# A routed two-layer block on one Trainium2 core: router logits taken from rows before their normalization

## The reference, cut to what matters

```python
def layer_norm(x, g, b):                       # float32
    mu = jnp.mean(xf, axis=-1, keepdims=True)
    var = jnp.mean(jnp.square(xf - mu), axis=-1, keepdims=True)
    y = (xf - mu) * lax.rsqrt(var + LN_EPS)
    return (y * g + b).astype(x.dtype)

# first block, for i in (0, 1); 256 tokens, D = 1024
h = x * (1.0 + sc_m) + sh_m
y = conformer_conv(h, ...) if i == 0 else short_gated_conv(h, ...)
x = layer_norm(ALPHA * x + (1.0 + g_m) * y, mix_ln_g[i], mix_ln_b[i])
h = x * (1.0 + sc_f) + sh_f
y = hierarchical_moe(h, ...)                   # 4 groups of 8 experts, D_EXPERT = 512
x = layer_norm(ALPHA * x + (1.0 + g_f) * y, ffn_ln_g[i], ffn_ln_b[i])

# hierarchical_moe
g_logits = xf @ w_group + b_group              # 4 columns
g_idx    = argmax(g_logits)
e_logits = (xf @ w_router + b_router)          # 32 columns, the 8 of the group are kept
top_p, top_e = lax.top_k(e_probs, 2)
# every expert: (silu(x @ w_gate) * (x @ w_up)) @ w_down, weighted and summed per token
```

## Time and profile before

| | us |
|---|---|
| median of 3 runs (2533.52 to 2539.37) | 2539.05 |
| span of the profiled execution, core 0 | 2539.9 |
| PE busy | 2433.0 (96%) |
| DVE busy | 1417.5 (56%) |
| ACT busy | 886.7 (35%) |
| POOL busy | 306.5 (12%) |
| PE's part of the chain that ended last | 74% |
| DMA's part of that chain | 15% |

### The profile page before, as it was taken

One profiled execution on the slowest core, in us unless ns is written; L12 is line 12 of the kernel. 1 busy time (PEld: TensorE's weight loads), 2 busy tenths in 40 slices (PEclk: granted clock), 3 DMA queues, 4 the chain that ended last, 5 costly groups with the idle time before them and its releaser, 6 DMA issues.

```text
span 2539.9 us, 37572 instructions
## 1 busy us (share of the span) xinstructions
PE 2433.0 (96%) x14976; PEld 1750.8 (69%) x14977; DVE 1417.5 (56%) x2512; ACT 886.7 (35%) x1560; POOL 306.5 (12%) x371
## 2 busy tenths in 40 slices
PE   7999999998999999998999999999999999999998
PEld 4664444443686444443488899988888889998887
DVE  6564323322666333323366785767677678576767
ACT  2241111111342111111144465454444446555443
POOL 0210001000000001000000122430010012243001
PEclk8999999999999999999999999999999999999999
DMA  9979999999887999999947563443743856345381
GB/s 396 380 307 418 419 420 419 419 419 419 293 302 296 408 420 419 419 420 419 399 138 269 164 192 115 140 169 127 271 166 127 271 163 190 114 140 171 123 274 52
DMA packets 246338, 710.44 MB, mean 280 GB/s; under 512 B 11794, under 2 KB 165138, under 8 KB 189586
## 3 DMA queue, kind: packets, MB, share of 16 engines
q1 hardware_dynamic: 243810, 704.94, 73.0%
q10 hardware_dynamic: 2352, 3.06, 0.4%
HBM read 705.46 MB, written 1.05 MB: 278 GB/s over the span
## 4 chain that ended last, share of the span: by engine, by line
PE 74%; DMA 15%; DVE 5%; issue 3%; ACT 2%; POOL 1%; SPq 0%; DVEq 0%; ACTq 0%; POOLq 0%
DMA ring<-in_e_w_up_dram 12%; PE w L1271 12%; PE y L1057 11%; PE w L1050 11%; PE w L975 8%; PE w L1289 6%; PE w L1049 6%; PE w L978 4%; PE w L1552 2%; PE w L1252 1%; PE y L1325 1%; PE y L876 1%; DVE wsp L1662 1%; PE y L1496 1%; ACT wsp L1652 1%
## 5 line engine op out<-in xcount | busy, mean ns | idle before, releaser
L1662 DVE TENSOR_TENSOR wsp<-ring,wsp 128x1024 fp32r<-128x1024 f32 x452 | 558.2, 1243 | 253.0 <-ACT wsp L1652 251.9
L1652 ACT CAST wsp<-ring 128x1024 fp32r<-128x1024 f32 x452 | 468.5, 1047 | 297.5 <-PE w L1050 99.4
L1271 PE MATMUL w<-ring,arena 128*64 128x512 f32 x2048 | 465.0, 601 | 47.3 <-DMA ring<-in_e_w_up_dram 45.0
L1271 PEld LDWEIGHTS w<-ring,arena 128*64 128x64 f32 x2048 | 151.1, 138 | 314.6 <-issue 308.0
L1050 PE MATMUL w<-hx,wsp 128*128 128x512 f32 x1344 | 348.2, 391 | 0.0
L1050 PEld LDWEIGHTS w<-hx,wsp 128*128 128x128 f32 x1344 | 246.9, 189 | 44.6
L975 PE MATMUL w<-hx,wsp 128*128 128x256 f32 x1984 | 266.2, 287 | 1.5 <-ACT arena L2801 1.1
L975 PEld LDWEIGHTS w<-hx,wsp 128*128 128x128 f32 x1984 | 248.4, 193 | 16.9 <-issue 12.3
L1057 PE MATMUL y<-wsp,zsp 128*128 128x512 f32 x1008 | 245.1, 392 | 2.9 <-POOL zsp L2910 1.7
L2164 DVE TENSOR_TENSOR ht<-w,ht 128x256 f32<-128x256 f32 x64 | 39.5, 618 | 370.8 <-ACT ht L2710 370.8
L2710 ACT ACTIVATE ht<-w 128x256 f32<-128x256 f32 x64 | 40.0, 626 | 586.7 <-PE w L1271 586.7
(11 more groups left out here) (351 smaller groups left out, 2938.7 us busy)
## 6 DMA issues: line engine op xcount, KB each, us to landing
ring<-in_e_w_gate_dram SPq DMA_DIRECT2D x128, 1024.0 KB, 13.6
ring<-in_e_w_up_dram SPq DMA_DIRECT2D x128, 1024.0 KB, 15.5
ring<-in_e_w_down_dram SPq DMA_DIRECT2D x112, 1024.0 KB, 13.6
ring<-in_ffn_in_dram SPq DMA_DIRECT2D x88, 1024.0 KB, 6.9
ring<-in_ada_w_dram SPq DMA_DIRECT2D x48, 1024.0 KB, 14.4
ring<-in_w_in_dram SPq DMA_DIRECT2D x48, 1024.0 KB, 5.4
ring<-in_ffn_out_dram SPq DMA_DIRECT2D x44, 1024.0 KB, 6.9
ring<-in_b_w_in_dram SPq DMA_DIRECT2D x12, 1024.0 KB, 12.2
```

Of the source, the lines that this page charges most:

```text
L1271: ins = pe.matmul(b[64 * c:64 * c + 64, :], xg[:, u, kc, x0:x0 + CAP], r4[:, k, :, 256 * c:256 * c + 256], start=kc == 0, stop=kc == KC - 1)
L1652: ac.copy(shaped(halves(i)[0], u.shape), u.cut(ring[:, u.piece % NSLOT, :])).then_inc(*mark("w_high", i))
L1662: ve.tensor_tensor(shaped(lo, u.shape), u.cut(ring[:, u.piece % NSLOT, :]), shaped(hi, u.shape).bitcast(F32), ALU.subtract).then_inc(*mark ...
```

## The change

Four things are rewritten, in both layers.

1. **Logits from raw rows.** PE transposes `vv` as soon as the residual has been added, not when it is normalized. The products with the 40 router columns then give logits of raw rows. With s and c the column sums (`router_sums`, 9 matmuls with 2 rows out) copied over all partitions (`router_rows`, 2 matmuls), logits are repaired on DVE by `base` = s * (-mean * rstd) + c and `fixed` = raw * rstd + `base`. The bias row's matmul for each block is gone. Scales of features (`router_scale`, the 16 small matmuls) stand behind the logits.
2. **Who normalizes.** DVE does no longer normalize; ACT does, as activation with scale and bias, two halves a block, followed by the two high parts of the block. Pool makes -mean * rstd behind each power, and then all four low parts. DVE has no `row_low` any more.
3. **DVE's order.** All four half rows are first gated and added, then statistics are taken. The steps of the choice of block 0 and 1 alternate. `negatives` is one instruction for a block. Of the scaling steps, `gathered(0, 1)` stands ahead of `token_weights`.
4. **PE's fillers.** In layer 0 no `ada(1,1,kc)` stands ahead of `moe(0)`: kc 0 and 1 stand behind the router, kc 2 to 4 behind the ranks of block 0, kc 5 to 7 behind the counts. In layer 1 `keep_busy` of 2, 5 and 4 stands at these places, and the one between the two blocks is gone.

The core of the diff:

```diff
             def router(l, n):
+                def turn_rows(t, h):
+                    pe.wait_ge(*at("norm_v", n, "added", t, h))
+                    for q in range(4):
+                        f = 4 * h + q
+                        ins = pe.transpose(WB[2 * t + h][:, q * P:(q + 1) * P], vv[:, t, f * P:(f + 1) * P], ident)
+                    ins.then_inc(*mark("route_pe", "turned", l, t, h))
+                turn_rows(0, 0)
+                turn_rows(0, 1)
+                router_sums(l, n)
+                turn_rows(1, 0)
+                router_rows(l)
+                turn_rows(1, 1)
...
+                router_scale(l)
...
                 if l == 0:
-                    for kc in range(4, 6):
+                    for kc in range(2):
                         ada(1, 1, kc)
                 else:
-                    keep_busy(WB[0], 4)
+                    keep_busy(WB[0], 2)
+                pe.wait_ge(*at("route_v", l, "oo", 0))
+                pe.matmul(b[:, 0:32], tri, oo[:, 0, :], start=True, stop=True).then_inc(*mark("route_pe", "ranks", l, 0))
+                if l == 0:
+                    for kc in range(2, 5):
+                        ada(1, 1, kc)
+                else:
+                    keep_busy(WB[0], 5)
...
-            router_shift(0)
-            for kc in range(4):
-                ada(1, 1, kc)
...
+                def base(t):
+                    ve.wait_ge(*at("route_s", "rows", l))
+                    ve.wait_ge(*at("shifted", n, t))
+                    step("base", t, lambda: ve.scalar_tensor_tensor(route_base[:, t, :], route_rows[:, 0, :], nm[:, t:t + 1],
+                                                                    route_rows[:, 1, :], ALU.mult, ALU.add))
...
+                def scaled(t, h):
+                    if h == 0:
+                        ac.wait_ge(*at("shifted", n, t))
+                    part = vv[:, t, h * 512:(h + 1) * 512]
+                    ac.activation(part, part, ACT.Identity, bias=nm[:, t:t + 1], scale=rs[:, t:t + 1]).then_inc(
+                        *mark("route_s", "scaled", l, t, h))
...
+            def row_lows(l, n):
+                for t in range(2):
+                    po.wait_ge(*at("rstd", n, t))
+                    po.tensor_scalar(nm[:, t:t + 1], mv[:, t, 0:1], rs[:, t:t + 1], -1.0, ALU.mult, ALU.mult).then_inc(*mark("shifted", n, t))
+                    if t == 0:
+                        norm_part(n, 1)
+                for t in range(2):
+                    for h in range(2):
+                        po.wait_ge(*at("route_s", "v_hi", l, t, h))
+                        po.tensor_tensor(in_chunks(vl[:, t, :])[:, h, :, :], by_four(vv[:, t, :])[:, h, :, :],
+                                         in_chunks(vh[:, t, :].bitcast(F32))[:, h, :, :], ALU.subtract).then_inc(*mark("v_lo", l, t, h))
```

More of the change, by code:

```diff
@@ L912, in to_feature_x, with router_sums, router_rows, router_scale @@
                             ins.then_inc(*mark("x_turned", f // 2))
-            def router_shift(l):
+            def router_sums(l, n):
                 pe.wait_ge(*at("route_v", "router", l))
+                pe.wait_ge(*at("norm_v", n, "gated", 1, 1))
+                o = YB[3][0:2, 208:248]
+                for kc in range(KC):
+                    pe.matmul(o, ab[:, 0:2, kc], wr[:, l, kc, :], start=kc == 0, stop=False)
+                pe.matmul(o, tri[0:1, 0:2], rb[:, l, :], start=False, stop=True).then_inc(*mark("route_pe", "sums", l))
+            def router_rows(l):
+                pe.wait_ge(*at("route_s", "two", l))
+                for v in range(2):
+                    ins = pe.matmul(YB[3][:, 128 + 40 * v:168 + 40 * v], ident[0:2, v:v + 1].to_broadcast([2, P]), route_two,
+                                    start=True, stop=True)
+                ins.then_inc(*mark("route_pe", "rows", l))
+            def router_scale(l):
+                pe.wait_ge(*at("route_s", "n_t", l, 1, 1))
                 o = WB[3][:, 64:80].rearrange("p (v g k) -> p v g k", v=2, g=2)
@@ L949, in router @@
-                    pe.wait_ge(*at("route_s", "row", l))
-                    pe.matmul(o, ones[0:1, :], rb[:, l, :], start=False, stop=True).then_inc(*mark("route_pe", "logits", l, t))
+                        ins = pe.matmul(o, n_t[:, t, kc, :], wr_n[:, kc, :], start=kc == 0, stop=kc == KC - 1)
+                    ins.then_inc(*mark("route_pe", "logits", l, t))
+                router_scale(l)
             def first_two_x(i):
@@ L1224, in moe @@
                 if l == 0:
-                    for kc in range(6, KC):
+                    for kc in range(5, KC):
                         ada(1, 1, kc)
+                else:
+                    keep_busy(WB[0], 4)
                 banks = [0]
@@ L2030, in slots, with rank @@
+                def rank(t, j):
+                    if j == 0:
+                        ve.wait_ge(*at("route_pe", "ranks", l, t))
+                    b, i = (YB[3], WB[1])[t], 2 * t + j
+                    step(f"rk{j}", t, lambda: ve.tensor_tensor_reduce(jk[:, i, :], oh_[:, t, j, :], b[:, 0:32], 1.0, 0.0,
+                                                                      ALU.mult, ALU.add, rk[:, i:i + 1]))
                 def slots(t):
@@ L2069, in moe @@
                 ve.wait_ge(*at("w_used", first["a_out" if l == 0 else "b_out"] + KC - 1))
-                row_low(0, 0)
-                groups(0)
-                best(0)
-                indices(0)
-                hits(0)
-                negatives(0)
-                row_low(1, 0)
-                ranks(0)
-                slots(0)
-                groups(1)
-                best(1)
-                indices(1)
-                hits(1)
+                base(0)
+                fixed(0)
+                gmax(0)
+                gidx(0)
+                gf(0)
+                penalty(0)
+                base(1)
+                within(0)
+                emax(0)
+                eidx(0)
+                ef_(0)
+                fixed(1)
+                hit(0, 0)
+                gmax(1)
+                hit(0, 1)
+                gidx(1)
+                both(0)
+                gf(1)
+                penalty(1)
+                within(1)
+                emax(1)
+                rank(0, 0)
+                eidx(1)
+                rank(0, 1)
+                ef_(1)
+                slots(0)
+                hit(1, 0)
+                hit(1, 1)
+                both(1)
+                negatives(0)
+                negatives(1)
                 choose(0, 0)
-                ranks(1)
+                rank(1, 0)
+                rank(1, 1)
                 slots(1)
                 choose(0, 1)
-                row_low(0, 1)
-                row_low(1, 1)
-                negatives(1)
                 prior[0] = ("sg0", 1)
```

159 lines of the change are left out of this document (75 added, 84 removed).

## The result

The kernel before took 2537.16 us in the median of 13 runs (2533.52 to 2540.17), the changed one 2542.20 us in the median of 13 (2536.35 to 2545.40). The medians are 5.0 us apart; the ratio estimated from all runs, which is used throughout, is 1.0015, with an interval of 1.0008 to 1.0022. That is 3.8 us slower (2.0 to 5.6), beyond the noise of the runs and within the 0.3% named in the prediction, where +2.0 us and 2541.0 (2533 to 2548) were forecast. The profiled execution has a span of 2540.6 us, that of the kernel before 2539.9. These two spans say less than the runs: the one before reached the end of the projection of layer 0 2.0 us later (168.95 against 166.99), and why it did no run here shows.

A forecast was written before the change was run, and what follows sets the result against it. DMA was taken to bound both expert layers, layer 1 paying by when `up(0)` starts. -1.5 us in layer 1 and +3.5 in layer 0 gave +2.0 on 2539.9; with the median 0.85 below, 2541.0 us, range 2533 to 2548.

The forecast's parts named there:

- The bounds: Both expert layers: DMA at about 420 GB/s bounds them; layer 0's router costs nothing, layer 1 gains by earlier `up(0)`.
- The signs it named: Layer 0 DMA standstill from 178 to 180-183; DVE steps of 1 to 2 us ending with Pool subtractions; layer 1 `up(0)` 795-798.
- The standstill in layer 0: Layer 0: moved `ada` reads delay expert pieces behind the router, so transfers stop; 2.0 to 5.2 us lost, 3.5 taken.
- case of full clock: Layer 0 with PE at full clock: 2.0 us lost, or 3.2 with DVE held up.
- The lock in layer 1: Layer 1's choice: four Pool subtractions of 1.7 us hold up DVE steps, costing 5.2 us and leaving 1.9 gained.
- The way without it: Layer 1 with nothing else in the way: gather starts at 787.0, `up(0)` at 790.9, 7.0 us gained.
- the rival's sum: Pool and DVE hardly meeting, at the lower clock: 3.8 us gained in layer 1, 5.1 lost in layer 0, +1.3.
- Fillers at the lower clock: Layer 1, between the ranks: five `keep_busy` take 4.4 us, not 2.5, putting `up(0)` at 797.7; 796.4 was taken.
- Layer 1 in all: Layer 1 up to `up(0)`: start at 796.4 instead of 797.92, 1.5 us gained.
- The free way: Rival: Pool's and DVE's steps hardly meet; layer 1 gains 7.0, layer 0 loses 2.0, total 2534; chance 0.20.
- The slower side: Rival, layer 1's choice: subtractions of 2.1 us or more and lower clock give +6.8 (2546) to +9 (2548); chance 0.20.

The follow-up runs named there:

- leaving-out run: The changed kernel with Pool's four subtractions in each layer replaced by fillings with zero, low parts not computed; ratio to the kernel before 0.9992 (0.9983 to 1.0001).
- fillers of 2, 2, 2: The changed kernel with kc 0 to 3 read ahead of `moe(0)`, low parts on DVE, layer 1 `keep_busy` 2, 2, 2 for 2, 5, 4; ratio 0.9979.
- 2, 2, 6: The kernel with fillers of 2, 2, 2, with layer 1's last `keep_busy` 6 instead of 2; ratio to the kernel before 0.9988 (0.9979 to 0.9997).
- four pieces ahead: The changed kernel with kc 0 to 3 of `ada(1,1)` read ahead of `moe(0)` in layer 0, as before the change; ratio 1.0009 (1.0000 to 1.0018).

## Why the prediction was right, point by point

- **The bounds.** That DMA bounds both layers, that nothing can be won in layer 0 and that layer 1 pays from `up(0)`: borne out by all twelve rows of the table. The forecast was +2.0 us, the runs give +3.8 (2.0 to 5.6). That 2541.0 lies so near 2542.20 is partly luck: it was counted from 2539.05, the median of 3 runs, and that of 13 is 2537.16.
- **The signs it named.** Layer 0 stands still for about 3 us, from 176.2 to 179.3 here, 178.2 to 181.3 when the execution's 2.0 us of lead are added. `up(0)` of layer 1 is at 799.72, 25.1 behind the projection, which is 796.8 where the projection ends at 771.69; 795 to 798 was said. Steps of 0.9 to 1.6 us end with Pool's subtractions.
- **The standstill in layer 0**, 3.5 us of 2.0 to 5.2. By transfers missing it is 4.1 us, by the stretch between the projections 4.9; where the other 0.8 comes from is open. The step held: the pieces run out about 9 us behind the projection (worked out: 177.8 - 168.95 = 8.9), and the clock does fall over the logits, which the forecast had only partly taken in (it chose 3.5, near the case of full clock). The same instructions with less of the lower clock, in the run with five fillers cut to two, had 3.0 missing. With 4.9 for 3.5 it is the largest part, 1.4, of the 1.8 us between forecast and result.
- **The lock in layer 1**, 5.2 us from 4 * (1.7 - 0.4). A subtraction takes 1.53 and 1.49, not 1.7; the four held steps are longer by 1.37, 0.73, 1.34 and 1.25 (against 0.18, 0.17, 0.24 and 0.17), 4.7 together. The leaving-out run gives 4.1 on the way to `up(0)`. The sums beside it are 0.1 to 0.2 off by their own terms (with 1.3 a subtraction 7.0 - 3.6 = 3.4 us are gained, with 2.1 it is 0.2), which changes nothing. Maxima, indices and `fixed` had been taken as free without a row: they are (0.16, 0.15). `TENSOR_SCALAR` and sums were rightly counted as held, with one exception below; the cast, which wasn't counted, is held too.
- **The way without it**, 7.0 us gained. With the subtractions left out it was 26.2 - 21.0 = 5.2. This term was too large by 1.8, and most of that is the clock: 7.0 is the sum at full clock, and in that run five fillers took 4.09, where 2.5 are taken at full clock. By the rival's sum 3.8 would be left at the lower clock, so the run lies between the two. That gather takes 4.0 and not 6.0 was put in without a word on why the 6.0 would fall away; it held (4.05) because the clock had come back by then. It is more than the whole gain of layer 1, as gather itself begins 0.8 us later than before.
- **Fillers at the lower clock.** At the lower level five were to take 4.4 us, from four in 3.50; they took 4.61, and the ranks of block 1 wait for them. The forecast had chosen a mean nearer to the full clock (796.4 between 796.0 and 797.7), and the lower level is what came.
- **Layer 1 in all**: 1.5 us earlier forecast, 1.1 measured. That these lie so close is partly luck, for two misses cancel: the lower clock puts `up(0)` at the forecast's own 797.7, 1.3 later than chosen, and four subtractions of 1.5 for 1.7 take 0.8 away, which gives 796.9 where 796.8 was measured. Small pieces missed each other: scaling on ACT 0.76 each and not 0.65, the product on Pool 0.26 and not 0.55.
- **The rivals.** The free way has its price shown by the leaving-out run (0.9992), and it isn't what happens. The slower side needed 2.1 us for a subtraction; it is 1.5.

The Trainium skill (SBUF — State Buffer, Who interferes with whom) had been quoted as agreeing. The traces bear out its finer part as well: a two-input DVE instruction contends with a GpSimd instruction that reads, not with one that only writes (1.55 beside a subtraction, 0.18 beside a filling), and casts and `TENSOR_SCALAR` are held by both (0.61 and 0.47 beside a filling of 0.53).

## What to carry to other kernels

Before work is moved ahead of the read of a buffer in a ring, ask what the transfer queue has left at that moment: where the first two pieces were read decided 4 to 9 us here, and no placing of the other six that was tried cost anything. Each long Pool instruction (1.5 us) beside a chain of small dependent DVE steps held one of them up by 0.7 to 1.4 us; the same work on DVE itself, at 1.07 us apiece, was cheaper than four times 1.5 on the "free" engine (`up(0)` at 22.7 and 22.9 against 23.9 to 25.1). And a filler is work like any other: where the clock had fallen anyway, four took 3.49 us for 1.97 and were what the next step waited for. Last, a gain or loss of 1 us in one profile is not a result while executions with the same instructions differ by as much.

## What the runs showed of the hardware

- A subtraction of 128x512, one input read with a step of four, takes 1.5 us on Pool and 1.07 on DVE; a filling of that size 0.53 on Pool. A product on 128x1 takes 0.26 on Pool, a power 0.55.
- A `TENSOR_SCALAR` on one column wasn't held: 0.15, twice, at 780.36 and 780.55, while a Pool subtraction ran (780.17 on). On two columns it took 1.44.
- Pool and DVE took turns. Where two Pool subtractions stood in a row, one DVE step of the held kind ran between them (the sum of 1.55 us in the changed kernel, a normalization in the kernel before with low parts on Pool), and four subtractions held four steps in the changed kernel.
- The same instructions in front (the two kernels with fillers of 2, 2, 2 and 2, 2, 6) were run at clock 1.00 and 0.50 at the same place of the program.
- Longer runs of a kernel tend to have the lower mean clock: of the eleven with four pieces ahead, the two with 0.990 took 2537.07 and 2538.45 us, the three with 0.986 took 2542.68 to 2544.66. Which is cause and which is effect, the list doesn't show.
